# Banded attention: the scores of two steps issued together in every even step, with a fourth buffer of probabilities

## What is computed

```python
def swa_sink_mixer(xn, w_in, sinks, w_out, t5_table):
    q, k, v, z = jnp.split(xn @ w_in, ...)
    o = banded_attention(q_heads(q), kv_heads(k), kv_heads(v), t5_table, 128, sinks)
    return (merge_heads(o) * jax.nn.silu(z)) @ w_out

# banded_attention, per block of 128 queries, with its own block of keys and the one before it
s = q @ k.T / 8 + bias[distance]
p = softmax(concat([s, sink]))[..., :-1]
o = p @ v
```

## Time and profile before

| what | value |
|---|---|
| median of the runs | 1234.31 us |
| the profiled execution's own time | 1234.64 us |
| its span, first to last instruction | 1232.8 us |
| PE busy | 1218.2 us, 99% of the span |
| DVE busy | 833.5 us, 68% |
| ACT busy | 495.4 us, 40% |
| mean granted TensorE clock | 0.999 of 2.4 GHz |
| the attention stage, steps 0 to 15 | from 1094.2 to about 1183 us of the span |

### The profile page before, as it was taken

How to read it: one execution, slowest core, us unless ns; L and a number is a source line. 1 busy time by engine, 2 the same in 40 slices (tenths; PEclk the granted TensorE clock), 3 DMA queues, 4 the chain that set the end, 5 groups by cost and what they waited for, 6 DMA issues and landing times.

```text
span 1232.8 us, 16256 instructions
## 1 busy us (share of the span) xinstructions
PE 1218.2 (99%) x5836; PEld 1008.1 (82%) x5836; DVE 833.5 (68%) x1272; ACT 495.4 (40%) x786; POOL 20.6 (2%) x24
## 2 busy tenths in 40 slices
PE   8999999999999999999999999999999999999998
PEld 7988888888888888888888888888888888877776
DVE  7848797797789987554357866666654444467874
ACT  7543333322333324642234533434433333155553
POOL 4000000000000000000000000000000000000000
PEclk9999999999999999999999999999999999999999
DMA  8432232222222232252322323322243534211111
GB/s 315 144 124 97 85 102 86 86 86 80 74 86 88 99 103 100 72 180 94 102 98 74 103 102 102 102 86 92 95 138 103 206 103 171 86 52 53 67 54 68
DMA packets 35762, 128.07 MB, mean 104 GB/s; under 512 B 4016, under 2 KB 5072, under 8 KB 35456
## 3 DMA queue, kind: packets, MB, share of 16 engines
q1 hardware_dynamic: 33120, 116.41, 28.1%
q0 software_dynamic: 1296, 8.62, 2.0%
q10 hardware_dynamic: 1296, 2.36, 0.5%
HBM read 125.25 MB, written 5.27 MB: 106 GB/s over the span
## 4 chain that ended last, share of the span: by engine, by line
PE 94%; DVE 3%; ACT 2%; issue 1%; DMA 1%; SPq 0%; DVEq 0%; ACTq 0%
PE acc L839 78%; PE acc L856 4%; PE acc L1172 1%; PE acc L909 1%; PE side L1172 1%; PE acc L1141 1%; DVE w_low L1206 1%; PE side L1112 1%; PE acc L873 1%; PE acc L1125 1%; PE side L978 1%; PE side L998 1%; DMA w_raw<-weights 1%; ACT w_high L463 0%; DVE x L1760 0%
## 5 line engine op out<-in xcount | busy, mean ns | idle before, releaser
L839 PE MATMUL acc<-h_high,w_high 128*128 128x512 f32 x880 | 342.8, 390 | 0.0
L839 PE MATMUL acc<-h_high,w_low 128*128 128x512 f32 x880 | 342.4, 389 | 0.0
L839 PE MATMUL acc<-h_low,w_high 128*128 128x512 f32 x880 | 342.4, 389 | 0.0
L1206 DVE TENSOR_TENSOR w_low<-w_raw,w_high 128x1024 fp32r<-128x1024 f32 x214 | 264.0, 1245 | 44.5 <-ACT w_high L463 41.3
L463 ACT ACTIVATE w_high<-w_raw 128x1024 fp32r<-128x1024 f32 x214 | 222.1, 1051 | 104.6 <-PE acc L839 91.0
L839 PEld LDWEIGHTS acc<-h_high,w_low 128*128 128x128 f32 x880 | 165.2, 188 | 34.3
L839 PEld LDWEIGHTS acc<-h_low,w_high 128*128 128x128 f32 x880 | 165.2, 188 | 34.2
L839 PEld LDWEIGHTS acc<-h_high,w_high 128*128 128x128 f32 x880 | 165.2, 188 | 34.0
L1274 DVE SCALAR_TENSOR_TENSOR convs<-long_u,par,convs 128x510 f32<-128x510 f32 (+28 forms) x232 | 170.3, 734 | 6.6
L839 PE MATMUL acc<-f_high,w_high 128*128 128x512 f32 x176 | 68.6, 390 | 0.0
L839 PE MATMUL acc<-f_low,w_high 128*128 128x512 f32 x176 | 68.5, 389 | 0.0
(11 more groups left out here) (314 smaller groups left out, 1894.6 us busy)
## 6 DMA issues: line engine op xcount, KB each, us to landing
w_raw<-weights SPq DMA_DIRECT2D x214, 512.0 KB, 3.2
rows_dram<-strip_dram POOLq DMA_DIRECT2D x1, 3072.0 KB, 14.9
x_in<-x SPq DMA_DIRECT2D x4, 512.0 KB, 7.7
x<-x POOLq DMA_DIRECT2D x1, 2048.0 KB, 8.6
bias<-rows_dram POOLq DMA_DIRECT2D x1, 2048.0 KB, 12.4
w_raw<-weights SPq DMA_DIRECT2D x8, 128.0 KB, 5.8
mem_in<-mem ACTq DMA_DIRECT2D x4, 256.0 KB, 6.6
out<-result SPq DMA_DIRECT2D x4, 256.0 KB, 2.0
```

The source lines that it names most:

```text
L839: mm = pe.matmul(acc[:, bank, 0:width], w[:, s, (skip + b) * P:(skip + b + 1) * P], moving[v][:, k, :], start=first and b == 0 and w is w_ ...
L1206: dve.tensor_tensor(w_low[:, s, :], raw[s][:, :], w_high[:, s, :].bitcast(F32), ALU.subtract)\
```

## The change

The two steps' scores that were issued one by one, `scores(step + 3)` after every `turn`, are issued in pairs: an even step issues `scores(step + 3)` and right behind it `scores(step + 4)`, an odd step none. The early `scores(0)`, `(1)` and `(2)` stay where they are. A fourth buffer of probabilities, `sw_probs3`, is added (it lies over `square` and `sum_sq`, which are free in the stage), with a fourth set of small columns; step t now uses number t % 4, and `biased(step)` waits for `turn(step - 4)` where it waited for `turn(step - 3)`. The condition in `scores` itself (the scores of `step - 2` have been read) is as before. The order on DVE, ACT and the queues of transfers is as before.

```diff
@@ buffers
-        sw_small = [small, sb("sw_small1", [P, 6, 4], F32), sb("sw_small2", [P, 6, 4], F32)]
+        sw_small = [small, sb("sw_small1", [P, 6, 4], F32), sb("sw_small2", [P, 6, 4], F32),
+                    sb("sw_small3", [P, 6, 4], F32)]
...
+        sw_probs.append(sb("sw_probs3", [P, 4, 2 * P], F32, square_at + 2))
@@ exps on ACT, turn on PE, biased and normalised on DVE
-                pr, sm = sw_probs[step % 3], sw_small[step % 3]
+                pr, sm = sw_probs[step % 4], sw_small[step % 4]
@@ the loop over steps on PE
             for step in range(2 * KT):
                 turn(step)
-                if step + 3 < 2 * KT:
-                    scores(step + 3)
+                if step % 2 == 0:
+                    for later in range(step + 3, min(step + 5, 2 * KT)):
+                        scores(later)
@@ biased on DVE
-                at_least(dve, sw_turned, step - 2)
+                at_least(dve, sw_turned, step - 3)
```

More of the change, by code:

```diff
@@ L1124, in turn @@
                     for r in range(4):
-                        mm = pe.transpose(acc[:, b, r * P:(r + 1) * P], sw_probs[step % 3][:, r, b * P:(b + 1) * P],
+                        mm = pe.transpose(acc[:, b, r * P:(r + 1) * P], sw_probs[step % 4][:, r, b * P:(b + 1) * P],
                                           ident)
```

## The result

| | before | after |
|---|---|---|
| median of 18 runs each | 1234.28 us (1233.93 to 1234.85) | 1235.92 us (1234.00 to 1237.61) |
| ratio, with its 95% interval | | 1.0014 [1.0007, 1.0020] |
| the profiled execution's own time | 1234.64 us | 1236.03 us |
| its span | 1232.8 us | 1234.2 us |

The change costs 0.14%, where a time 0.1 us under that of before was forecast, and the runs scatter over 3.6 us where those of before keep within 1 us. The scatter has an order. By the mean granted clock of the span they fall into three groups: three runs with 0.999 took 1234.0 to 1234.2 us, eight with 0.998 took 1235.5 to 1236.1, seven with 0.997 took 1236.7 to 1237.6.

What follows compares the result with a forecast made beforehand. TensorE (PE), 99% busy, was taken to bound the kernel. Step 0's loss of +1.92 us less the pairs' 2.07 us gave -0.15 us, so 1234.2 us against the median, with a range from 1233.0 to 1236.9 us.

Steps and rivals of the forecast that it cites:

- The saving of a pair: Later attention steps: joining two steps' scores saves PE 0.42 us, or 0.39 us with narrow moved scores; together 2.07 us.
- The rule of the Trainium skill: Paired scores: about 60 cycles overhead per matmul would cut a pair's saving to 0.22 us, the sum 1 us higher.
- The wait of step 0: Before `scores(4)`: PE idles some 3.0 us for DVE's `biased(2)`, until 1098.7; `outputs(0)` starts 1.9 us (1.92) late.
- the old wait before `outputs(0)`: PE's existing idle stretch before `outputs(0)`: takes up 0.8 us of the delay from step 0, then no wait there.
- rival 1: TensorE's clock falls in step 0's wait, slowing the product behind it: 1236.9 us with one such product; chance 0.11.
- The price of the rival: Product behind step 0's wait: 12 matmuls 0.46 us apart instead of 0.23, +2.75 us for one such product.
- Joined batches do not cost what two cost: Rival 2, in the pairs: a joined batch costs what two batches cost, leaving only step 0's loss: 1236.2 us; chance 0.10.
- no joined batch waits for DVE after step 0: Rival 4, every even step: DVE becomes late and joined batches wait; 1239.2 us with 1 us each; chance 0.04.
- the wait of step 0 is not absorbed whole: Rival 3, ahead of `outputs(0)`: step 0's wait is absent or absorbed whole by the ACT and DVE chain: 1232.2 us; chance 0.05.
- The fourth buffer: DVE's `biased(4)`: keeps late `turn(1)` from holding it up by a few tenths; worth 0 us either way.
- The tie before `outputs(2)`: ACT's copy ends at 1125.91, PE starts `outputs(2)` at 1126.33: a tie, up to 0.1 us may be lost.

Runs made afterwards that it cites:

- experiment 1: Changed kernel with pairs issued only from step 2 on, steps 0 and 1 as in the kernel before: 1232.77 us, ratio 0.9986 to the kernel before.
- Experiment 6: Changed kernel with scores 4 put behind the first 6 of the 12 matmuls of step 0's product: 1232.90 us, ratio 0.9988 to the kernel before.
- experiment 3: Changed kernel with twelve matmuls of unread result put into the wait of step 0, ahead of scores 4: 1234.59 us, ratio 1.0000 to the kernel before.
- experiments 4: Changed kernel with scores issued in every step as before, keeping the four buffers and looser DVE wait: 1234.51 us, ratio 1.0001 to the kernel before.
- experiment 8: Changed kernel with the three buffers and tighter DVE wait of before: 1235.83 us, ratio 1.0009 to the kernel before.
- 9: Kernel of experiment 7 with the three buffers and tighter DVE wait of before: 1231.82 us, ratio 0.9977 to the kernel before.
- experiment 7: Kernel of experiment 1 with ACT's copy of turn 1 moved ahead of exps 3: 1232.12 us, ratio 0.9981 to the kernel before.

## Why the prediction was wrong

**The saving of a pair** was right: 0.42 us and 0.39 us from the distances within a batch gave 2.07 us, and the trace shows 2.05; the medians of experiment 1 and of before show 1.8. The rule of the Trainium skill that was weighed there, "TensorEngine Tiling (Array Packing)", "Instruction Overhead", with its cycles per matmul, would have left 1.1 us of it; the second scores of step 2 cost 0.86 us, which leaves it no room.

**The wait of step 0** was right in place, length and cause: 2.86 us, ended at 1098.67 by line 1685 of `biased(2)` on DVE (the row names `sw_small`, the small column in which that line leaves its maximum), and so were the 0.8 us that fall into the old wait before `outputs(0)`. Experiment 6 moved the wait and the same counting held in the trace; experiment 3 kept it and gave 1234.59 us against 1234.58 before, where 1.92 - 2.07 say 0.15 us less.

**What failed is the step from there to the forecast: that TensorE keeps its clock through the wait.** It was told as rival 1 with a chance of 0.11, on the ground that the only fall in the trace came after 4 us of idling and that 3.0 us are less. By the runs it is the usual case here: 15 of 18 are slower than the forecast by 1.3 to 3.4 us, and the profiled one, at 1236.03 us close to the median, shows the clock at 0.55 behind the wait. The one row at the end of the kernel was taken for a limit. It is not one: it tells when the clock fell once, in one execution, after a dense stretch. The same place in two other kernels, whose end is the same work, shows how far this moves (experiment 1, then experiment 3):

```profile
1224.00:1229.00 5.00, 0.35 (x2) 0.00 (x0) 2.86 (x7) 2.38 (x6) 0.00 (x0) 1.00 0.45 168
1229.00:1230.00 1.00, 0.00 (x0) 0.00 (x0) 0.00 (x0) 0.00 (x0) 0.00 (x0) 0.85 0.56 211
```

```profile
1226.00:1228.00 2.00, 0.89 (x4) 0.39 (x3) 1.93 (x4) 1.00 (x4) 0.00 (x0) 1.00 0.59 224
1228.80:1228.90 0.10, 0.00 (x0) 0.00 (x0) 0.08 (x1) 0.00 (x0) 0.00 (x0) 1.00 0.00 0
1228.90:1229.00 0.10, 0.00 (x0) 0.00 (x0) 0.09 (x1) 0.00 (x0) 0.00 (x0) 0.50 0.00 0
```

In experiment 1 PE stops at 1224.35 and the clock falls at 1229.7, after 5.4 us of idling; in experiment 3 PE stops at 1226.89 and the clock falls at 1228.9, after 2.0 us. In step 0 the idling comes after 0.7 us of idling and 1.6 us of short work, and PE was busy in 1.64 of 4.50 us. What the clock does there varies from run to run. The Trainium skill, "TensorE: Matmul & The Clock Gate", Part 1, has the clock halved after idling and restored after sustained work; the changed kernel's trace agrees, in its rows from 1098.67 to 1102.57, with a lower level from 1099.1 to 1102.5.

**The price of the rival** was sized wrong too. It was put at a whole product of 12 matmuls at half speed, 2.75 us. In the trace it is 1.6 us, which fits 3.4 us at half the clock (1.7 us): 1.67 - 1.06 = 0.6 us on `scores(4)` and 1.0 us on the product: from its first matmul to `turn(1)` are 1104.19 - 1100.34 = 3.85 us, and 2.85 us in experiment 3's kernel, where the clock held (1100.03 to 1102.88). The group of runs at 1236.7 to 1237.6 lost about twice that; none of them was profiled, and that their clock stayed low for twice as long is read from the mean alone (0.997 against 0.998 and 0.999).

**The other rivals** did not come. Joined batches do not cost what two cost; no joined batch waits for DVE after step 0; and the wait of step 0 is not absorbed whole. The fourth buffer is worth nothing, as said (experiments 4, 8 and 9), though the wait that it hides on DVE is 1.94 us, by the trace of experiment 8, and not a few tenths.

**The tie before `outputs(2)`** is a tie: after, `outputs(2)` starts 0.37 us behind the last matmul of its product, at 1129.04, where 0.32 us was the distance before.

Whether the wait alone or the short work ahead of it as well makes the fall is settled only in part. Filling the wait removes the falls (experiment 3) with the short work left in place, so the idling is needed in this place. That the short work helps was not tried, by an equal wait behind dense work for instance. Nor is the length at which falls begin sharp: with 2.9 us idle 15 of 18, 8 of 11 and 6 of 6 runs show them by time and clock, with 1.7 us 2 of 11, and with 1.3 us (experiment 6) at most one, at 1233.8 us.

## What to carry to other kernels

Joining two batches that need the same setting of the array saved 0.4 us a pair, and this could be counted beforehand from the starts of the records, not from their lengths. Before issuing a step earlier on the bounding engine, look up for its first and last occurrences too when the other engine frees the operand: here five of six moves were free and the sixth cost nearly as much as the five gave (1.9 of 2.1 us), before the clock took 1.6 us more. An idle stretch of a few microseconds on TensorE has to be priced at its length plus the slow stretch behind it, and if runs of a kernel scatter by more than those of its neighbour, the granted clock of each run is the first thing to compare.

## What the runs showed that was not expected

- TensorE's clock can fall behind 2.9 us of idling in most executions (in the profiled one 0.4 us after the idling had ended), and the same program in the same place keeps it in others: 3 of 18 runs of the changed kernel were at 1234.0 to 1234.2 us. At the end of the kernel it fell after 2.0 us of idling in one trace and after 5.4 us in another.
- Work that computes nothing can pay: twelve matmuls put into the wait brought the median from 1235.92 to 1234.59 us (ratios to the kernel before 1.0014 and 1.0000), four of them to 1234.49.
- A wait on PE of 1.3 us costs 0.6 us by the trace (experiment 6 against 1), as the delay that it makes is taken up in part by the wait before `outputs(0)`; and where no wait stands ahead of that one, removing it (experiment 7 against 1) gives 0.65 us.
